# Halved norms of a two-block transformer: square sums in one matmul a slot later, two roundings moved on ScalarE, tap blocks started four slots later

## The reference

```python
for layer in range(DEPTH):                       # a: short conv + forgetting attention, b: conformer
    u = rms_norm(h, norm_mix_pre[layer])
    m = mixer(u)                                 # ends in an out projection
    h = h + rms_norm(m, norm_mix_post[layer])
    f = swiglu_ffn(rms_norm(h, norm_ffn_pre[layer]), w_ffn_in[layer], w_ffn_out[layer])
    h = h + rms_norm(f, norm_ffn_post[layer])
...
def rms_norm(x, g):
    y = xf * lax.rsqrt(jnp.mean(xf * xf, axis=-1, keepdims=True) + RMS_EPS)
```

## Time and profile before

| what | value |
|---|---|
| median of 3 runs | 2433.08 us (2430.32 to 2433.72) |
| the profiled execution | 2434.33 us, of it the span 2432.5 us |
| busy: TensorE | 2364.1 us, 97% |
| busy: VectorE, ScalarE, GpSimd | 1313.0, 866.8, 23.9 us |
| mean granted TensorE clock | 0.992 |
| DMA | 216.30 MB, mean 89 GB/s |

### The profile page before, as it was taken

The page is one execution under the profiler, slowest core; times in us unless marked ns, Lnnn a source line. Parts: engine busy times, 40 slices in busy tenths (PEclk is TensorE's granted clock), DMA queues, the critical chain, the costliest instruction groups (busy, mean ns, idle before and its releaser), DMA issues.

```text
span 2432.5 us, 32810 instructions
## 1 busy us (share of the span) xinstructions
PE 2364.1 (97%) x12314; PEld 1963.0 (81%) x12314; DVE 1313.0 (54%) x2017; ACT 866.8 (36%) x1314; POOL 23.9 (1%) x16
## 2 busy tenths in 40 slices
PE   8999999999898999999999999999999989999997
PEld 6888888889764888888988987888888777888886
DVE  6564655523534564542366585666623895666523
ACT  6444422222423532222342254333322564333322
POOL 0000000000110000000000000000000000000000
PEclk9999999999999999999999999999999999999999
DMA  4112222222362232222222111222222212222222
GB/s 155 61 61 85 80 99 99 95 95 82 93 174 80 70 104 95 95 95 95 87 91 78 44 57 58 96 98 100 95 95 95 72 36 70 104 96 101 97 95 78
DMA packets 68013, 216.30 MB, mean 89 GB/s; under 512 B 11600, under 2 KB 12112, under 8 KB 67920
## 3 DMA queue, kind: packets, MB, share of 16 engines
q1 hardware_dynamic: 67632, 214.63, 26.3%
q10 hardware_dynamic: 288, 0.36, 0.1%
HBM read 210.64 MB, written 4.33 MB: 88 GB/s over the span
## 4 chain that ended last, share of the span: by engine, by line
PE 86%; DVE 7%; ACT 4%; issue 1%; DMA 1%; SPq 0%; DVEq 0%; ACTq 0%
PE bank L443 25%; PE bank L445 24%; PE bank L444 24%; PE bank L855 2%; PE bank L770 2%; PE bank L642 1%; PE bank L641 1%; PE bank L643 1%; DVE w_lo L1492 1%; ACT w_hi L1015 1%; ACT ds L1444 1%; DVE h L1553 1%; DVE m L1548 1%; DVE acc L1521 1%; DVE small L2101 1%
## 5 line engine op out<-in xcount | busy, mean ns | idle before, releaser
L1015 ACT ACTIVATE w_hi<-raw 128x1024 fp32r<-128x1024 f32 x378 | 400.3, 1059 | 1171.4 <-PE bank L445 1043.1
L443 PE MATMUL bank<-u_hi,w_hi 128*128 128x512 f32 (+1 forms) x2088 | 795.5, 381 | 11.1 <-DVE w_lo L1492 4.6
L445 PE MATMUL bank<-u_hi,w_lo 128*128 128x512 f32 (+1 forms) x2088 | 786.8, 377 | 0.0
L444 PE MATMUL bank<-u_lo,w_hi 128*128 128x512 f32 (+1 forms) x2088 | 786.7, 377 | 0.0
L1492 DVE TENSOR_TENSOR w_lo<-raw,w_hi 128x1024 fp32r<-128x1024 f32 x378 | 462.6, 1225 | 413.5 <-ACT w_hi L1015 413.0
L443 PEld LDWEIGHTS bank<-u_hi,w_hi 128*128 128x128 f32 x2088 | 394.3, 189 | 91.4 <-issue 13.1
L445 PEld LDWEIGHTS bank<-u_hi,w_lo 128*128 128x128 f32 x2088 | 393.8, 189 | 72.4
L444 PEld LDWEIGHTS bank<-u_lo,w_hi 128*128 128x128 f32 x2088 | 394.5, 189 | 71.4 <-issue 1.2
L443 PE MATMUL bank<-hid_hi,w_hi 128*128 (+1 forms) x528 | 208.0, 394 | 0.0
L445 PE MATMUL bank<-hid_hi,w_lo 128*128 (+1 forms) x528 | 207.0, 392 | 0.0
L444 PE MATMUL bank<-hid_lo,w_hi 128*128 (+1 forms) x528 | 204.9, 388 | 0.0
(11 more groups left out here) (287 smaller groups left out, 2590.4 us busy)
## 6 DMA issues: line engine op xcount, KB each, us to landing
raw<-weights_dram SPq DMA_DIRECT2D x378, 512.0 KB, 3.2
bz<-gated_dram SPq DMA_DIRECT2D x32, 270.0 KB, 4.9
gated_dram<-bz SPq DMA_DIRECT2D x8, 272.0 KB, 2.1
h<-x_t_dram SPq DMA_DIRECT2D x8, 256.0 KB, 6.6
out_dram<-m SPq DMA_DIRECT2D x8, 256.0 KB, 2.2
ap<-select_dram SPq DMA_DIRECT2D x1, 512.0 KB, 8.7
vec<-vectors_dram SPq DMA_DIRECT2D x1, 343.0 KB, 7.6
cmask<-masks_dram ACTq DMA_DIRECT2D x1, 224.0 KB, 2.6
```

Source lines behind the costliest of these rows:

```text
L443: pe.matmul(out, wh, xh, start=start, stop=False)
L444: pe.matmul(out, wh, xl, start=False, stop=False)
L445: return pe.matmul(out, wl, xh, start=False, stop=stop)
L1015: act.activation(w_hi[:, j, :], raw[:, j, :], ACT.Copy).then_inc(hi_ready, 1)
```

## The change

Seven edits, all at the four boundaries but the last:

- VectorE now adds the squares of both pairs to `acc` (`add_pair` takes a pair), so `post_sums` is one matmul instead of three.
- The sums of half 0 stand later: in `halved_out` at the second chunk, k = 4 (before: first chunk, k = 3); in `back_halved` at the second slot, c = 1 (before: first slot, c = 2).
- The sums of half 1 stand later: in the second input chunk, k = 4 (before: first input chunk, k = 3).
- ScalarE rounds `w_hi` of slot s+2 ahead of the second root, and of slot s+3 right behind it (before: both behind it, the second behind two `u_hi`).
- In the `f` boundaries ScalarE keeps pair 0 of half 1 after a new count of `out_half`, ahead of its wait for the slot.
- The waits of `keep_pair` go by the count of `acc_ready` alone.
- GpSimd waits for slot `b_in` + 4 before the first tap block.

```diff
-ACC, _ = starts([(s, KC - 2 if s == "final" else KC - 1) for s in STATS])
+ACC, _ = starts([(s, KC - 2 if s == "final" else 3 + 2 * 4 if s in POSTS else KC - 1) for s in STATS])
...
             pool.wait_ge(taps_landed, 16 * SHIFTS * (GROUPS + 1))
+            pool.wait_ge(slot_done, SLOT["b_in"] + 4)
...
-                    if between and k == 3:
+                    if between and k == 4:
                         between()
...
             def post_sums(stat, half):
 
                 to = stat_bank(stat, half)[:, tokens(half)]
-                pe.wait_ge(acc_ready, ACC[stat] + 5 + 2 * half)
-                pe.matmul(to, ones[:, :], acc[:, tokens(half)], start=True, stop=False)
-                pe.wait_ge(sq_ready, SQ[stat] + 6 + 2 * half)
-                pe.matmul(to, ones[:, :], sq[:, 1, 0:HT], start=False, stop=False)
-                pe.matmul(to, ones[:, :], sq[:, 1, HT:T], start=False, stop=True).then_inc(sum_full, 1)
+                pe.wait_ge(acc_ready, ACC[stat] + 3 + 4 * (half + 1))
+                pe.matmul(to, ones[:, :], acc[:, tokens(half)], start=True, stop=True).then_inc(sum_full, 1)
...
-                               between=(lambda: post_sums(stat, 0)) if n == 0 else None).then_inc(slot_done, 1)
+                               between=(lambda: post_sums(stat, 0)) if n == 1 else None).then_inc(slot_done, 1)
...
-                                          between=(lambda: post_sums(stat, 1)) if n + half == 0 else None)
+                                          between=(lambda: post_sums(stat, 1)) if half == 0 and n == 1 else None)
...
-                        if between and c == 2:
+                        if between and c == 1:
                             between()
...
-                            back_halved(n, (1,), (lambda: post_sums(f"{l}_fpost", 0)) if n == HALF - 4 else None)
+                            back_halved(n, (1,), (lambda: post_sums(f"{l}_fpost", 0)) if n == HALF - 3 else None)
...
-                if half and pair:
-                    act.wait_ge(sum_full, SUM[stat] + 1)
+                if half:
+                    act.wait_ge(acc_ready, ACC[stat] + 5 + 2 * pair)
                 else:
-                    act.wait_ge(acc_ready, ACC[stat] + (5 if half else 2 + pair))
+                    act.wait_ge(acc_ready, ACC[stat] + 2 + pair)
...
+                if "f" in stat:
+                    act.wait_ge(out_half, OUT_HALF[made] + 3)
+                    keep_pair(stat, 1, 0)
                 act.wait_ge(slot_done, s)
-                if "f" in stat:
-                    keep_pair(stat, 1, 0)
                 keep_pair(stat, 1, 1)
+                high_part(s + 2)
                 half_root(stat, 1)
-                high_part(s + 2)
-                half_input(stat, 1, range(2))
                 high_part(s + 3)
-                half_input(stat, 1, range(2, KC))
+                half_input(stat, 1, range(KC))
...
-                add_pair(stat, 0)
+                for pair in range(2):
+                    add_pair(stat, 0, pair)
                 half_norm(stat, 0, {3: s, 5: s + 1})
                 if "f" in stat:
-                    add_pair(stat, 1)
+                    add_pair(stat, 1, 0)
+                add_pair(stat, 1, 1)
                 low_part(s + 2)
                 half_norm(stat, 1, {1: s + 3})
```

More of the change, by code:

```diff
@@ L104 @@
 MADE, _ = starts([(s, KC + 4) for s in MADE_IN])
-OUT_HALF, _ = starts([(s, 2) for s in MADE_IN])
+OUT_HALF, _ = starts([(s, 3 if "ffn" in s else 2) for s in MADE_IN])
 FULL, _ = starts([(s, 3 if s in "ab" else 6) for s in "abcd"])
@@ L643, in back_halved @@
                                 last = pe.matmul(out, ws[1], xh, start=False, stop=final, skip_group_check=True)
-                        if halves == (0,) and n == HALF - 1 and c % 2:
+                        if n == HALF - 1 and (c == 1 or c == 3 and halves == (0,)):
                             last.then_inc(out_half, 1)
@@ L1527, in scaled_low, with add_pair @@
                                          op0=ALU.mult, op1=ALU.subtract).then_inc(u_ready, 1)
-            def add_pair(stat, half):
+            def add_pair(stat, half, pair):
                 t = tokens(half)
+                dve.wait_ge(sq_ready, SQ[stat] + 5 + 2 * half + pair)
                 for i in range(2):
[L1533 to L1536, removed]
+                    n = ACC[stat] + 3 + 4 * half + 2 * pair + i
+                    dve.wait_ge(acc_ready, n if pair + i else ACC[stat] + 3)
+                    dve.tensor_tensor(acc[:, t], acc[:, t], sq[:, pair, tokens(i)], ALU.add).then_inc(acc_ready, 1)
             def half_norm(stat, half, low_after):
```

## The result

The changed kernel takes **2421.98 us** (median of 6 runs, 2420.29 to 2422.87) against 2433.4 us for the kernel before in the same comparison (6 runs, 2430.32 to 2436.56). The ratio is 0.9952, with a 95% interval of 0.9942 to 0.9963. The forecast was 2422.1, in a range from 2419.0 to 2427.0.

What follows compares the result with a forecast made beforehand. TensorE, busy 97% of the span, was taken as the bound, so only its work and waits count. +0.25 + 0.25 - 2.7 - 9.3 + 0.5 = -11.0 us from the median of 2433.08 gave 2422.1, range 2419.0 to 2427.0.

Steps and rivals of the forecast that it cites:

- The sum: Whole kernel: the terms of the four boundaries and the tap blocks' new place add to -11.0 us, chance 0.70.
- b_fpost: Boundary where the third `m` was to come at 1217.6 against 1220.47; taken as 2.7 us earlier.
- a_fpost: Boundary to gain the same 2.7 us as `b_fpost` plus 6.6 of the tap blocks: 9.3 us earlier.
- the 6.62 us between the two `f` boundaries: Extra length of `a_fpost` over `b_fpost`, first input matmul to pre-norm's sum; laid to GpSimd's tap blocks, about 1.15 to clock.
- The later first sum costs: In `a_post`, the first root comes 2.3 us later, opening a 3.3 us TensorE wait at the first input chunk.
- a_post: Boundary to end 0.25 us later: later sums nearly paid back by the roundings, saved matmul time going into waits.
- The roundings pay: In `a_post`, the chain from the second Exp's end to the third `m` falls from 7.1 to 2.94 us.
- the slower rival: All four boundaries: later sums not paid back, second root's chain stays 7.1 us long; 2438.1 us, chance 0.03.
- the clock rival: TensorE's clock halves at the two new 3.3 us waits, each costing up to 1.15; 2424.4 us, chance 0.14.
- The step that missed: `b_post` with convolution and layer norm: +0.75 us, from +0.25 as in `a_post` and 0.5 for `bz` held.

## Why the prediction was right

**The sum.** It came out as -11.4 us by the medians of one comparison, for -11.0, and as -12.0 by the two profiled executions. Two of its terms are confirmed by themselves: `b_fpost` at -2.86 for -2.7, and `a_fpost` at -9.51 for -9.3. That the 6.62 us between the two `f` boundaries would go was right, but not all of it was the tap blocks': taken alone the tap edit makes the stage 5.3 us shorter, since 1.15 of the 6.62 was the clock behind the 3.04 us wait, which that kernel keeps. The prediction named the 1.15 as the clock but did not say that it needs the wait to go. The full change removes both, so the sum held.

**The later first sum costs.** The wait was forecast at 3.3 us and read 2.98 at `a_post`, 3.27 at `b_post`, and 1.17 at both `f` boundaries for 1.3. The experiment without it shows that it cost 6 us in all. By the prediction's own rows the 3.3 should have been 3.1 (TensorE comes at 240.72 - 0.86 = 239.86, and not at 239.7), nearer to what was measured.

**The roundings pay.** 7.08 us behind the second root with the old order, 2.97 with the new, from the end of the Exp (251.37) to the third `m` (254.34):

```profile
250.95 0.42 ACT L1072 ACTIVATE rs<-rs 128x256 f32<-128x256 f32 x1
```

Undone, the kernel is slower than before by 6 us, near the 2438.1 of the slower rival.

**a_post.** +0.46 for +0.25. Three costs and gains nearly cancel here. The experiments have each: the roundings -4.1, the later first sum +2.7, the one-matmul sums at the old places +1.9, in sum +0.5. The clock did fall there: in the windows view the granted clock of 244 to 248 is 0.62.

```profile
240.00:244.00 4.00, 1.02 (x10) 0.84 (x8) 3.27 (x6) 1.94 (x4) 0.00 (x0) 1.00 0.60 216
244.00:248.00 4.00, 4.00 (x23) 4.00 (x24) 3.27 (x7) 3.53 (x7) 0.00 (x0) 0.62 0.01 4
```

So the clock rival's condition, which had 0.14, came true, at `b_post` too (0.72 in 828 to 834), and its 2424.4 did not. Its price was hidden, as argued: the second sum came at 249.81, which is 0.25 later than the working gives when moved by the 1.06 us by which this execution ran late. The half-speed matmuls ran in the time that would have been two short waits: from the first input matmul to the pre-norm's sum it is 23.23 and 23.12 us at `a_post` and `b_post`, no more than the 23.35 of the `f` boundaries, where the clock stayed up. There was luck in this. With the tap blocks behind the first `bz` the half clock at `b_post` lasted twice as long, from 825.3 to 832.2; the second sum stood 7.10 us behind the first input matmul instead of 5.77, and the boundary took 24.45 us, 1.3 more.

**The step that missed** is `b_post` with its lead-in: -0.48 for +0.75. The first convolution came +0.40 later. The boundary itself took +0.1: from its first sum of squares to the pre-norm's sum it is 37.13 us before (823.36 to 860.49) and 34.05 after (817.97 to 852.02), and the first sum stands 3.2 us of matmuls later in the program.

```profile
823.36 0.60 PE L536 MATMUL bank<-acc,ones 128*128 128x256 f32 x2
```

```profile
817.97 0.60 PE L537 MATMUL bank<-acc,ones 128*128 128x256 f32 x2
```

What is left, -1.0, lies between, where the change touches nothing. The layer norm there gave more than that. Before:

```profile
774.51 1.10 PE L787 MATMUL bank<-bsum,ones 128*128 128x512 f32 x2 [1.64 <-DVE bsum L1818]
775.82 1.97 PE L789 MATMUL bank<-acc,ones 128*128 128x512 f32 x2 [0.21 <-DVE acc L1825]
777.59 1.91 PE L791 MATMUL bank<-by,ones 128*128 128x512 f32 x2
...
784.86 1.19 PE L470 MATMUL bank<-by_hi,w_hi 128*128 128x512 f32 x2 [4.50 <-ACT by_hi L1321]
```

After:

```profile
766.95 1.10 PE L785 MATMUL bank<-bsum,ones 128*128 128x512 f32 x2 [1.64 <-DVE bsum L1818]
768.26 1.13 PE L787 MATMUL bank<-acc,ones 128*128 128x512 f32 x2 [0.21 <-DVE acc L1825]
769.22 1.02 PE L789 MATMUL bank<-by,ones 128*128 128x512 f32 x2
...
775.59 1.19 PE L471 MATMUL bank<-by_hi,w_hi 128*128 128x512 f32 x2 [4.50 <-ACT by_hi L1319]
```

The same two matmuls take 1.97 and 1.91 us in one kernel and 1.13 and 1.02 in the other, at half and at full speed, after the same waits. From `bsum` to `by_hi` it is 10.35 and 8.64 us: -1.71. Behind the 4.50 us wait the clock is at half in both, for 0.5 us longer in the changed kernel, which costs it +0.24. Another +0.44 lies in the matmuls of 256 columns ahead of the first sum, which stand 0.118 us apart where they stood 0.1135 before; why is open. So about 1 us of the gain between the two profiles is not the change's. Without it the stage would be at about +0.55, near its forecast of +0.75.

Whether the clock has fallen in the layer norm differs between the profiles: in three of the eleven (the kernel before, the early first sums, the roundings only) it is at half there, and the stage is 1.7 us longer for it. The stage's length in the nine experiments' profiles goes from 211.28 to 219.18, and only part of that follows from the edits.

## What to carry to other kernels

When work is moved later to spare an engine a wait, follow what hangs on it all the way round: here the wait came back, larger, one chunk on, and a second edit (two roundings taken off the path behind the root) had to pay for it. Ask of each edit alone what it gives; here an edit that cost 6 us was hidden behind one that gave 17 (2439.39 - 2421.98), and that one gave 9.5 in the kernel before, where there was less to pay back. Two passages of the same program that differ in length are the cheapest experiment there is: subtract one from the other and look for what runs beside only one.

## What was not expected of the hardware

- After the same idle time TensorE's clock fell in one passage and not in the other. 3.04 us idle in `a_fpost` was followed by half speed in the kernel before, and 3.04 us in `b_fpost` was not. With the tap edit alone both were, the second 1.4 us late; with the roundings alone 3.03 us in `a_fpost` was not, and 3.03 us in `b_fpost` was. The 2.98 us in `a_post` and the 3.27 in `b_post` were followed by it in all five kernels that have them. Shorter ones can be too: 1.89 us in `a_post` with the roundings back (half clock from 254.2), and 1.64 us at the layer norm in three kernels of eleven. The length of the idle stretch alone does not tell.
- Moving the tap blocks out of one VectorE passage into another costs there too: one `w_lo` 2.40 us for 1.22, and 2.70 with the blocks behind `bz`. TensorE waits 0.28 us for it, and that was free only because it waits for `bz` soon after in any case.
- How much of the spread between the stages is the clock was larger than expected: the layer norm alone makes 1.7 us.
